# Moving sums, low halves and a table load in the weight stream of a transformer block

## The chip, the cores and the metric

The kernel runs on one core of one Trainium2 chip. The metric is the device time of one execution in microseconds. TensorE is called PE below, VectorE DVE, ScalarE ACT, GpSimd POOL and SyncE SP, as the profile does.

## What is computed

Two blocks in a row over 512 tokens of width 1024, in float32. All that matters for this change lies in the first part of the first block:

```python
mod = c_act @ w_ada[l] + b_ada[l]          # 6 vectors of 1024; c_act = silu(c)
shift1, scale1, gate1, shift2, scale2, gate2 = jnp.split(mod, N_MOD, axis=-1)
h = modulate(rms_norm(x, norm1_g[l]), shift1, scale1)
proj = h @ w_in[l]
q, k, v, g_ret, u, sv, gate_a, gate_b = jnp.split(proj, IN_SPLITS, axis=-1)
q = rotary(q, pos); k = rotary(k, pos)     # heads, scale of k left out
y_ret = head_norm(retention(q, k, v), ret_gn_g[l])
branch_a = (jax.nn.silu(g_ret) * y_ret) @ w_ret_out[l]
y_sgu = spatial_gating(gelu(u), gelu(sv), ...)
branch_b = y_sgu @ w_sgu_out[l]
merged = sigmoid(gate_a) * branch_a + sigmoid(gate_b) * branch_b
x = x + gate1[:, None, :] * (merged @ w_out[l])
```

After it come a lookup among 16384 experts (most of the time) and a second block of two layers, whose own modulation vectors (two conditions, `c_2` and `c_ctx_2`) are products of the same kind with `w_mod`.

## The kernel before

**Weight stream.** All weights come as chunks of 128 by 1024 floats (512 KB), in one order that `make_plan` writes down, and SP loads them one by one into a ring `WR` of `SLOTS` = 4 places. `load(n)` (L641) waits until chunk n-4 has been used. There are two kinds of chunk. A *product chunk* (a "split" in the code) is taken apart for PE: ACT writes its rounded high half `WH` (`high`, L1205) and DVE the rest `WL` (`low`, L1623); after that its place in `WR` is free (`w_split`). `WH` and `WL` have four places of their own, which are free when PE has finished with them. Each product is three matmuls, high by high, high by low and low by high. A *modulation chunk* holds 128 outputs of a modulation vector and never goes to PE: DVE multiplies it by the condition and sums (`mod_sums`, L1635), after which its place is free (`mod_used`). The first 48 of the 96 modulation chunks take one such instruction each, the others two (L1641 and L1643), since they serve two conditions.

**Order of the stream.** 16 modulation chunks come first, since `h` needs shift1 and scale1. The others are strewn between the product chunks by `p.mod(...)` in the plan: one behind each of the eight `qk` chunks, two behind each of the eight `v` chunks, two behind each of the first four `sv` chunks and one behind each of the last four, one behind each chunk of `g_ret`, `u`, `gate_a`, `ret_out`, `gate_b` and `sgu_out`, until 96 are reached. The stages are worked off in this order by PE. `v` and `sv` (function `token_rows`) work in four pairs: a pair of chunks is multiplied with all 512 tokens in four banks, and needs both of its chunks taken apart. Between `v` and `sv` stand the retention scores `s` and values `y`, which need no chunk.

**Order on an engine.** Every engine runs its instructions in the order of the code. Before ACT or DVE reads the bank of a job, `ahead` makes it take all chunks apart up to two behind the newest product chunk of that job (`LOOK` = 2). So the `high` of both chunks of the next `v` pair stands on ACT ahead of its reads of this pair, and the `low` of the first two `sv` chunks stands on DVE ahead of the scores. `streamed(n)` is what DVE does for product chunk n, in this order: the sums of all modulation chunks that lie before it in the stream, then its `low`.

**Start.** ACT's queue asks for the condition `cond`, the vectors `vec`, four constants (`small_loaded`) and the input `XT`; after the squares for the norm it asks for the rotary and decay tables (`tab`, 1.5 MB, L1270), then takes the first two product chunks apart and waits for the scales (`mod_ready`) before it writes `XW` and `Hh` (`shift`, L1256 and L1259). DVE waits for `vec` and the constants before its first sum, sums the 16 chunks with parts of the norm between them (`scaled`, L1714), adds the bias (`biased`), makes `scl1`, and then takes apart two chunks and writes `Hl` (`lowered`, L1720). PE begins with `together` (L813), the first two `qk` chunks at once, as the eight tiles of `Hh` and `Hl` come.

Of the kernel before, what the change touches and what calls it, by code (L numbers as in the profile page):

```python
# [8 lines left out]
T = 512  # L9
C = 256  # L10
A = T + C
KD = D // P
# [16 lines left out]
SPREAD = (1, 2, 3, 0)  # L29
SLOTS = 4  # L30
LOOK = 2
MODS, MODS1 = 96, 48
HOTS = 4
TN = 384
SPARSE, DENSE = 3, (0, 1, 2)
# [123 lines left out]
def make_plan():  # L159
    p = Plan()  # L160

    def lin(key, what, owner, n, cols=("x",)):
        for f in range(n):
            p.chunk((key, f), (*what, f))
            for c in cols:
                p.job((key, f, c), owner, [(key, f)] if c == cols[-1] else [])
# [12 lines left out]
            p.job((*key, "to", g), "V" if g in SPREAD[2:] else "A")  # L179

    p.limit = -1
    p.mod(16)
    p.job(("norm1",), "A")
    spreads(("norm1",))
    p.limit = np.inf

    for f in range(10):
        if f < 8:
            p.chunk(("qk", f), ("w_in", 0, f))
            p.mod()  # L190
            p.job(("qk", f), "A", [("qk", f)])
        if f >= 2:
            p.job(("qkp", f - 2), "V")
# [13 lines left out]
    for name, at in (("g_ret", 2048), ("u", 3072)):  # L207
        for f in range(8):
            p.chunk((name, f), ("w_in", at, f))
            p.mod()  # L210
            p.job((name, f, "x"), "A", [(name, f)])
            if name == "g_ret" and f == 1:
                for h in range(RET_H):
                    p.job(("spread", h), "V")
    for f in range(8):
        p.job(("mix", f), "V")
    for gate, at, name in (("gate_a", 5120, "ret_out"), ("gate_b", 6144, "sgu_out")):
        for f in range(9):
# [4 lines left out]
            if f:  # L223
                p.chunk((name, f - 1), ("w_" + name, 0, f - 1))
                p.mod()
                p.job((name, f - 1, "x"), "V", [(name, f - 1)])
    lin("w_out", ("w_out", 0), "V", 8)
    p.job(("norm2",), "A")
    spreads(("norm2",))
    for f in range(17):  # L230
# [187 lines left out]
def build(nc, plan, d, out):  # L418
# [9 lines left out]
    with ctx:  # L428
# [757 lines left out]
        def _(act):  # L1186
# [80 lines left out]
            act.wait_ge(x_loaded, k.at(x_loaded, 16))  # L1267
            for j in range(KD):
                square(XT, XW, j, T)
            dma(tab[:, 0:3072], d["tab1"][:, :]).then_inc(tab_loaded, 16)  # L1270
            root(("norm1",), rt, T, D)
            spread_norm(("norm1",), rt, T)
            for n in range(LOOK):
                high(n)
            split[0] = LOOK
            act.wait_ge(mod_ready, k.next(mod_ready))
            shift(XW, Hh, lambda c, j: scl1[:, j:j + 1], lambda c, j: mod[:, j, 0:1], ("x",), T)
            for dst, src in ((bs, "bs"), (ws.rearrange("p g t -> p (g t)"), "ws"), (lng[:, :], "lng"), (lnb[:, :], "lnb")):
# [334 lines left out]
        def _(dve):  # L1613
# [4 lines left out]
            def low(n):  # L1618

                dve.wait_ge(w_hi, k.at(w_hi, n + 1))  # L1620
                if n >= SLOTS:
                    dve.wait_ge(*k.emptied(filled, v_used, n))
                v.tensor_tensor(WL[:, n % SLOTS, :, :].rearrange("p a b -> p (a b)"),  # L1623
                                WR[:, plan.splits[n] % SLOTS, :, :].rearrange("p a b -> p (a b)"),
                                WH[:, n % SLOTS, :, :].rearrange("p a b -> p (a b)").bitcast(f32),
                                ALU.subtract).then_inc(w_split, k.inc(w_split))
# [20 lines left out]

            def streamed(n):

                while summed_mods[0] < MODS and plan.mods[summed_mods[0]] < plan.splits[n]:  # L1650
                    mod_sums(summed_mods[0])
                    summed_mods[0] += 1
                low(n)

            def ahead(key):

# [26 lines left out]
            for n, g in ((0, 3), (1, 2), (1, 3)):  # L1683
                v.memset(epsx[QUAD * g:QUAD * (g + 1), n:n + 1], QUAD * QUAD * EPS).then_inc(dve_step, k.inc(dve_step))
            dve.wait_ge(vec_loaded, 16)
            dve.wait_ge(small_loaded, k.at(small_loaded, 16 * len(CONSTS)))

            def biased(lo, hi):

                dve.wait_ge(mod_used, hi)  # L1690
                if lo < MODS1:
                    m, bias = mod[:, lo:hi, 0], V("bias", lo, hi - lo)
                else:
                    m, bias = mod[:, lo:hi, 1:3], V("bias", lo, hi - lo).unsqueeze(2).to_broadcast([P, hi - lo, 2])
                v.tensor_tensor(m, m, bias, ALU.add).then_inc(dve_step, k.inc(dve_step))
                dve.wait_ge(*k.own())
# [15 lines left out]
            def scaled(j, x, work, w):  # L1712

                v.tensor_tensor(work[:, j, 0:w], x[:, j, 0:w], rt[:, 0:w], ALU.mult)\  # L1714
                    .then_inc(xr_ready, k.inc(xr_ready))

            def lowered(j, work, hi, lo, w):

                dve.wait_ge(t_hi, k.next(t_hi))
                v.tensor_tensor(lo[:, j, 0:w], work[:, j, 0:w], hi[:, j, 0:w].bitcast(f32),  # L1720
                                ALU.subtract).then_inc(h_ready, k.inc(h_ready))
# [8 lines left out]
                    if j >= 3:  # L1730
                        lowered(j - 3, work, hi, lo, w)

            for f in range(16):
                mod_sums(f)
                summed_mods[0] += 1
                if f == NORM1_AT:
                    inverted(("norm1",), rt, T)
                if f == NORM1_AT + 1:
                    spread_norm(("norm1",), rt, T)
                if f > NORM1_AT + 1:  # L1740
                    scaled(f - NORM1_AT - 2, XT, XW, T)
            biased(0, 16)
            v1(scl1[:, :], mod[:, 8:16, 0], 1.0, V("norm1", 0, 8), ALU.add, ALU.mult)\
                .then_inc(mod_ready, k.inc(mod_ready))
            for j in range(16 - NORM1_AT - 2, KD):
                scaled(j, XT, XW, T)
            for n in range(LOOK):
                streamed(n)
            split[0] = LOOK
            for j in range(KD):  # L1750
                lowered(j, XW, Hh, Hl, T)

            dve.wait_ge(tab_loaded, k.at(tab_loaded, 16))
            for f in range(8):
# [755 lines left out]
```

## Time and profile before

| | us |
|---|---|
| median of 3 runs | 3556.45 (3555.76 to 3560.99) |
| the profiled execution | 3556.28 |
| its span in the trace | 3554.4 |
| PE busy | 3404.8 |
| DVE busy | 2224.8 |
| ACT busy | 1471.7 |
| POOL busy | 631.4 |

The profile's times are those of one execution, counted from the start of its span. A page of the profile shows the busy time of each engine, the chain of work that ended last, and the costliest groups of instructions. The trace behind it can be read instruction by instruction, and for every one it names what ended the idle time before it. The first 560 us are the part of the first block that the change touches.

### The profile page before, as it was taken

To read this page: it belongs to the slowest core of one execution; us is meant where nothing else is said; L and a number is where in the kernel's file an instruction comes from. 1 tells how busy PE (TensorE), PEld (TensorE's weight loads), DVE (VectorE), ACT (ScalarE), POOL (GpSimd) and SP (SyncE) were. 2 spreads that over 40 slices of the span, in tenths; PEclk is the share of its full clock that TensorE was granted. 3 is DMA by queue.
4 is the path that set the end of the run, shared out by engine and by line. 5 is a ranking of instruction groups with operands and counts; after the bars stand their busy time and mean duration, and the time that the engine had idled before them with its cause. 6 is when DMAs were issued, how large, how long until landed. Compare 5 with 4: busy or idle time off the path is not lost.

```text
span 3554.4 us, 51348 instructions
## 1 busy us (share of the span) xinstructions
PE 3404.8 (96%) x19633; PEld 2956.6 (83%) x19633; DVE 2224.8 (63%) x4546; ACT 1471.7 (41%) x2577; POOL 631.4 (18%) x549
## 2 busy tenths in 40 slices
PE   5999999999999999999999999999999889999997
PEld 4878887999999999999986678778888666777886
DVE  6587765799896668888873652473333346447443
ACT  3233234356767643333343541362122345435222
POOL 0000000037788834443410000000000000000000
PEclk8999999999999999999999999999999899999999
DMA  7545643379889999999952012101221311221222
GB/s 276 194 144 168 202 146 113 115 234 301 293 290 340 293 323 387 361 354 377 390 209 77 31 43 71 37 19 60 66 66 54 114 46 36 78 66 43 94 96 101
DMA packets 219874, 595.84 MB, mean 168 GB/s; under 512 B 17776, under 2 KB 101360, under 8 KB 216176
## 3 DMA queue, kind: packets, MB, share of 16 engines
q1 hardware_dynamic: 159312, 405.84, 33.3%
q0 software_dynamic: 36864, 134.23, 10.9%
q10 hardware_dynamic: 23456, 52.48, 3.9%
q8 instruction: 158, 2.59, 0.3%
q14 instruction: 84, 0.69, 0.1%
HBM read 531.67 MB, written 60.82 MB: 167 GB/s over the span
## 4 chain that ended last, share of the span: by engine, by line
PE 89%; DVE 6%; DMA 2%; ACT 1%; issue 1%; POOL 0%; ACTq 0%; DVEq 0%
PE bank L788 66%; PE bank L988 14%; PE bank L1112 2%; PE bank L957 2%; PE bank L1098 2%; PE bank L813 1%; DMA rows<-in_urows,rk 1%; DMA WR<-in_weights 0%; PE bank L875 0%; DVE SrowA L2214 0%; DVE WL L1623 0%; DVE X L2362 0%; PE bank L945 0%; DVE OF L2359 0%; ACT X2W L1256 0%
## 5 line engine op out<-in xcount | busy, mean ns | idle before, releaser
L1623 DVE TENSOR_TENSOR WL<-WR,WH 128x1024 fp32r<-128x1024 f32 x512 | 628.3, 1228 | 540.0 <-ACT WH L1205 484.9
L1205 ACT ACTIVATE WH<-WR 128x1024 fp32r<-128x1024 f32 x512 | 538.2, 1059 | 580.1 <-PE bank L988 294.2
L788 PE MATMUL bank<-H2h,WH 128*128 128x512 f32 (+1 forms) x1624 | 579.3, 357 | 4.5 <-DVE H2l L1676 4.5
L788 PE MATMUL bank<-H2h,WL 128*128 128x512 f32 (+1 forms) x1624 | 574.5, 354 | 0.0
L788 PE MATMUL bank<-H2l,WH 128*128 128x512 f32 (+1 forms) x1624 | 573.9, 353 | 0.0
L788 PE MATMUL bank<-Hh,WH 128*128 128x384 f32 (+1 forms) x1440 | 517.7, 359 | 5.8 <-DVE WL L1623 5.8
L788 PE MATMUL bank<-Hh,WL 128*128 128x384 f32 (+1 forms) x1440 | 505.7, 351 | 0.0
L788 PE MATMUL bank<-Hl,WH 128*128 128x384 f32 (+1 forms) x1440 | 505.6, 351 | 0.0
L988 PE MATMUL bank<-ah,WH 128*128 128x384 f32 x1024 | 344.4, 336 | 9.0 <-issue 4.5
L788 PEld LDWEIGHTS bank<-H2h,WH 128*128 128x128 f32 x1624 | 308.4, 190 | 50.1 <-issue 7.7
L788 PEld LDWEIGHTS bank<-H2h,WL 128*128 128x128 f32 x1624 | 308.4, 190 | 43.5 <-issue 1.9
L988 PE MATMUL bank<-al,WH 128*128 128x384 f32 x1024 | 344.0, 336 | 0.0
L988 PE MATMUL bank<-ah,WL 128*128 128x384 f32 x1024 | 343.9, 336 | 0.0
L788 PEld LDWEIGHTS bank<-H2l,WH 128*128 128x128 f32 x1624 | 307.8, 190 | 42.3
L719 POOL DMA_INDIRECT rows<-in_urows,rk x128 | 157.8, 1233 | 847.0 <-DVE rk L2026 656.7
L788 PEld LDWEIGHTS bank<-Hh,WH 128*128 128x128 f32 x1440 | 271.6, 189 | 25.3 <-DVE WL L1623 6.7
L788 PEld LDWEIGHTS bank<-Hh,WL 128*128 128x128 f32 x1440 | 271.6, 189 | 16.8 <-issue 1.2
L788 PEld LDWEIGHTS bank<-Hl,WH 128*128 128x128 f32 x1440 | 271.1, 188 | 16.5
L735 POOL TENSOR_SCALAR hotB<-iota,KT 128x128 f32<-128x128 f32 x288 | 283.8, 997 | 2.8
L719 POOL DMA_INDIRECT rows<-in_vrows,rk x128 | 188.9, 1476 | 278.4 <-DVE acc L2043 254.7
L988 PEld LDWEIGHTS bank<-ah,WH 128*128 128x128 f32 x1024 | 193.6, 189 | 10.4 <-issue 5.9
L988 PEld LDWEIGHTS bank<-ah,WL 128*128 128x128 f32 x1024 | 193.5, 189 | 0.0
(363 smaller groups left out, 5557.3 us busy)
## 6 DMA issues: line engine op xcount, KB each, us to landing
WR<-in_weights SPq DMA_DIRECT2D x498, 512.0 KB
WR<-in_vrows SPq DMA_DIRECT2D x128, 512.0 KB
gelu_by_expert<-geU ACTq DMA_DIRECT2D x128, 192.0 KB
gates_by_expert<-tab SPq DMA_DIRECT2D x24, 1024.0 KB
geV<-gelu_by_expert SPq DMA_DIRECT2D x32, 768.0 KB
Gt<-gates_by_expert SPq DMA_DIRECT2D x14, 1536.0 KB
x_kept<-X ACTq DMA_DIRECT2D x2, 3072.0 KB, 10.5
X<-x_kept ACTq DMA_DIRECT2D x2, 3072.0 KB, 12.0
```

The source lines that it names most:

```text
L719: nc.gpsimd.indirect_dma_start(rows[:, i % ROWS, :], None, d[table][:, :], bass.IndirectOffsetOnAxis(ap=expert[:, pick:pick + 1].bitcast(u ...
L735: nc.gpsimd.tensor_scalar(hotB[:, n % HOTS, t, :], consts["iota128"][:, :], KT[:, tt % 2, 1, c:c + 1], None, ALU.is_equal)\
L788: yield nc.tensor.matmul(b[0:rows, out_cols], a, r, start=n == 0, stop=n == len(pairs) - 1)
L813: last = nc.tensor.matmul(b, a, r, start=j == 0 and n == 0, stop=j == KD - 1 and n == 2)
L957: yield nc.tensor.matmul(col(b, t), hotB[:, n % HOTS, t, :], hotA[:, n % HOTS, t, :], start=True, stop=True)
L988: mm = nc.tensor.matmul(bank[sums[dd].bank][:, 0:TN], a, r, start=c == 0 and n == 0, stop=c == NK - 1 and n == 2)
L1098: yield nc.tensor.transpose(col(b, t - t0), col(Srow[kind][u % 4], t), consts["ident"][:, :])
L1112: yield nc.tensor.matmul(b[p0:p0 + VB, 0:P], v_[:, t, 0:VB], PT[kind][:, u % 2, n_, :], start=n_ < 2, stop=n_ >= len(tiles) - 2)
L1205: act.activation(WH[:, n % SLOTS, :, :].rearrange("p a b -> p (a b)"), WR[:, c % SLOTS, :, :].rearrange("p a b -> p (a b)"), ACT.Copy)\
L1623: v.tensor_tensor(WL[:, n % SLOTS, :, :].rearrange("p a b -> p (a b)"), WR[:, plan.splits[n] % SLOTS, :, :].rearrange("p a b -> p (a b)"), ...
```

## The change

Nothing is computed otherwise. Four things move.

1. `streamed(n)`: the `low` of product chunk n comes before the sums of the modulation chunks that lie ahead of it in the stream.
2. The plan: the first product chunk goes ahead of the 16th modulation chunk, the second right behind that; the modulation chunks behind the first two `qk` chunks and behind the first six `g_ret` chunks are gone from there. They come later, since the numbering just runs on: `v` has sums 22 to 37 (24 to 39 before), `sv` 38 to 49 (40 to 51), `g_ret` 50 and 51 (52 to 59), `u` 52 to 59 (60 to 67), the last four places of the `gate_b` stage carry one again, and so do the first four `w_out` chunks. Sums from number 48 on are the double ones, so `sv` has two of them where it had four.
3. DVE's start: it waits for `vec` alone before the first sum, for the constants only after `Hl` is written. `low(0)` and two `scaled` stand ahead of the 16th sum; the other six `scaled` are strewn between the `lowered`.
4. ACT's start: `tab` is asked for behind `high(0)` and `high(1)`.

```diff
-    p.mod(16)
+    p.mod(MODS0 - 1)
     p.job(("norm1",), "A")
...
+    p.chunk(("qk", 0), ("w_in", 0, 0))
+    p.mod()
+    p.chunk(("qk", 1), ("w_in", 0, 1))
     for f in range(10):
         if f < 8:
-            p.chunk(("qk", f), ("w_in", 0, f))
-            p.mod()
+            if f >= 2:
+                p.chunk(("qk", f), ("w_in", 0, f))
+                p.mod()
...
             p.chunk((name, f), ("w_in", at, f))
-            p.mod()
+            if name == "u" or f >= 6:
+                p.mod()
...
-    lin("w_out", ("w_out", 0), "V", 8)
+    for f in range(8):
+        p.chunk(("w_out", f), ("w_out", 0, f))
+        p.mod()
+        p.job(("w_out", f, "x"), "V", [("w_out", f)])
...
-            dma(tab[:, 0:3072], d["tab1"][:, :]).then_inc(tab_loaded, 16)
             root(("norm1",), rt, T, D)
             spread_norm(("norm1",), rt, T)
             for n in range(LOOK):
                 high(n)
             split[0] = LOOK
+            dma(tab[:, 0:3072], d["tab1"][:, :]).then_inc(tab_loaded, 16)
             act.wait_ge(mod_ready, k.next(mod_ready))
...
             def streamed(n):
 
+                low(n)
                 while summed_mods[0] < MODS and plan.mods[summed_mods[0]] < plan.splits[n]:
                     mod_sums(summed_mods[0])
                     summed_mods[0] += 1
-                low(n)
...
             dve.wait_ge(vec_loaded, 16)
-            dve.wait_ge(small_loaded, k.at(small_loaded, 16 * len(CONSTS)))
...
-            for f in range(16):
+            for f in range(MODS0):
+                if f == MODS0 - 1:
+                    for j in range(2):
+                        scaled(j, XT, XW, T)
+                    low(0)
                 mod_sums(f)
...
-                if f > NORM1_AT + 1:
-                    scaled(f - NORM1_AT - 2, XT, XW, T)
-            biased(0, 16)
+            biased(0, MODS0)
             v1(scl1[:, :], mod[:, 8:16, 0], 1.0, V("norm1", 0, 8), ALU.add, ALU.mult)\
                 .then_inc(mod_ready, k.inc(mod_ready))
-            for j in range(16 - NORM1_AT - 2, KD):
-                scaled(j, XT, XW, T)
-            for n in range(LOOK):
-                streamed(n)
+            low(1)
             split[0] = LOOK
             for j in range(KD):
+                if j + 2 < KD:
+                    scaled(j + 2, XT, XW, T)
                 lowered(j, XW, Hh, Hl, T)
+            dve.wait_ge(small_loaded, k.at(small_loaded, 16 * len(CONSTS)))
```

What stands in a row on DVE at the start, before the change, from the eleventh sum to the first writes of `Hl` (L1635 are the sums, L1623 the low halves, L1714 `scaled`, L1720 `lowered`):

```order
L1635 SCALAR_TENSOR_TENSOR WR,mod<-WR,cond 128x1024
L1714 TENSOR_TENSOR XW<-XT,rt 128x512
L1695 TENSOR_TENSOR mod<-mod,vec 128x16
L1743 SCALAR_TENSOR_TENSOR scl<-mod,vec 128x8
L1714 TENSOR_TENSOR XW<-XT,rt 128x512 x3
L1623 TENSOR_TENSOR WL<-WR,WH 128x1024
L1635 SCALAR_TENSOR_TENSOR WR,mod<-WR,cond 128x1024
L1623 TENSOR_TENSOR WL<-WR,WH 128x1024
L1720 TENSOR_TENSOR Hl<-XW,Hh 128x512 x8
```

And with the change (sums now L1643, low halves L1631, `scaled` L1721, `lowered` L1727):

```order
L1643 SCALAR_TENSOR_TENSOR WR,mod<-WR,cond 128x1024 x4
L1721 TENSOR_TENSOR XW<-XT,rt 128x512 x2
L1631 TENSOR_TENSOR WL<-WR,WH 128x1024
L1643 SCALAR_TENSOR_TENSOR WR,mod<-WR,cond 128x1024
L1702 TENSOR_TENSOR mod<-mod,vec 128x16
L1752 SCALAR_TENSOR_TENSOR scl<-mod,vec 128x8
L1631 TENSOR_TENSOR WL<-WR,WH 128x1024
L1721 TENSOR_TENSOR XW<-XT,rt 128x512
L1727 TENSOR_TENSOR Hl<-XW,Hh 128x512
```

The 17th sum is gone from this place, and the scales (`scl`) stand behind three `scaled` less and one low half more.

DVE in the `v` stage before the change, where it comes from the last rotary product of `kT` (L1762):

```order
L1762 TENSOR_TENSOR kT<-kT,G_63 128x512
L1635 SCALAR_TENSOR_TENSOR WR,mod<-WR,cond 128x1024 x2
L1623 TENSOR_TENSOR WL<-WR,WH 128x1024
L1635 SCALAR_TENSOR_TENSOR WR,mod<-WR,cond 128x1024 x2
L1623 TENSOR_TENSOR WL<-WR,WH 128x1024
```

The same place with the change (L1771 is the rotary product):

```order
L1771 TENSOR_TENSOR kT<-kT,G_63 128x512
L1631 TENSOR_TENSOR WL<-WR,WH 128x1024
L1643 SCALAR_TENSOR_TENSOR WR,mod<-WR,cond 128x1024 x2
L1631 TENSOR_TENSOR WL<-WR,WH 128x1024
L1643 SCALAR_TENSOR_TENSOR WR,mod<-WR,cond 128x1024 x2
```

The pair of sums that freed two places of the ring ahead of a low half now stands behind it, eight times in a row here.

DVE at the head of the `g_ret` stage before the change, behind the reciprocal of the variances (L1797); `SV`, `yT` and `lng` are the normalised rows, the retention output and a gain:

```order
L1797 RECIPROCAL ST<-ST 128x512
L1641 SCALAR_TENSOR_TENSOR unread,mod<-WR,tab 128x1024
L1643 SCALAR_TENSOR_TENSOR WR,mod<-WR,tab 128x1024
L1623 TENSOR_TENSOR WL<-WR,WH 128x1024
L1801 TENSOR_TENSOR SV<-SV,lng 128x1024 x4
L1641 SCALAR_TENSOR_TENSOR unread,mod<-WR,tab 128x1024
L1643 SCALAR_TENSOR_TENSOR WR,mod<-WR,tab 128x1024
L1623 TENSOR_TENSOR WL<-WR,WH 128x1024
L1808 SCALAR_TENSOR_TENSOR yT_61<-yT_61,vec,bank 128x512 x8
```

With the change:

```order
L1806 RECIPROCAL ST<-ST 128x512
L1631 TENSOR_TENSOR WL<-WR,WH 128x1024
L1810 TENSOR_TENSOR SV<-SV,lng 128x1024 x4
L1631 TENSOR_TENSOR WL<-WR,WH 128x1024
L1817 SCALAR_TENSOR_TENSOR yT_61<-yT_61,vec,bank 128x512 x8
```

Four of these double-length sum instructions are gone from here, and two more behind.

## Rows read from the trace of the kernel before

**Rows 1.** the page's head: span, and busy time, share of the span and instructions of PE.

```profile
span 3554.4 us, 51348 instructions
PE 3404.8 (96%) x19633; PEld 2956.6 (83%) x19633; DVE 2224.8 (63%) x4546; ACT 1471.7 (41%) x2577; POOL 631.4 (18%) x549
```

**Rows 2.** timeline of the start; start us, us, engine line op out<-in [idle before <-what ended it].

```profile
11.35 1.23 DVE L1635 SCALAR_TENSOR_TENSOR WR<-WR,cond 128x1024 f32<-128x1024 f32 x1 [9.88 <-DMA iota<-in_consts]
...
16.07 0.35 ACTq L1270 DMA_DIRECT2D tab<-in_tab  x1
...
40.44 0.17 DVE L1743 SCALAR_TENSOR_TENSOR scl<-mod,vec 128x8 f32<-128x8 f32 x1
...
42.99 1.06 ACT L1205 ACTIVATE WH<-WR 128x1024 fp32r<-128x1024 f32 x1 [2.79 <-DMA WR<-in_weights]
...
46.58 0.77 PE L813 MATMUL bank<-Hh,WH 128*128 128x512 f32 x1 [15.76 <-DVE Hl L1720]
```

**Rows 3.** a 5 us window; busy PE, PEld, DVE, ACT, POOL, granted PE clock, DMA share, GB/s.

```profile
25.00:30.00 5.00, 0.00 (x0) 0.00 (x0) 4.60 (x8) 0.00 (x0) 0.00 (x0) 0.50 0.99 358
```

**Rows 4.** DMA issues of the first 100 us; KB each, median us to landing.

```profile
tab<-in_tab ACTq DMA_DIRECT2D x1, 1536.0 KB, 9.4
vec<-in_vec ACTq DMA_DIRECT2D x1, 105.0 KB, 6.7
```

**Rows 5.** timeline of the v stage, DVE first, then ACT; columns as in rows 2.

```profile
104.04 0.09 DVE L1635 DVE_READ_ACCUMULATOR WR<-WR,cond 128x1 f32 x1
105.19 0.09 DVE L1635 DVE_READ_ACCUMULATOR WR<-WR,cond 128x1 f32 x1
108.06 1.23 DVE L1635 SCALAR_TENSOR_TENSOR WR<-WR,cond 128x1024 f32<-128x1024 f32 x1 [0.50 <-DMA WR<-in_weights]
...
124.06 0.08 DVE L1635 DVE_READ_ACCUMULATOR WR<-WR,cond 128x1 f32 x1
...
109.86 1.06 ACT L1205 ACTIVATE WH<-WR 128x1024 fp32r<-128x1024 f32 x1 [8.66 <-DMA WR<-in_weights]
130.97 1.06 ACT L1205 ACTIVATE WH<-WR 128x1024 fp32r<-128x1024 f32 x1 [5.57 <-DMA WR<-in_weights]
```

**Rows 6.** chain of work that ended last; start us, us, what.

```profile
105.30 4.54 DMA WR<-in_weights
...
112.28 34.80 PE bank L788 x288
147.11 0.39 ACT Vr L1231
```

**Rows 7.** timeline of DVE in the sv stage; columns as in rows 2.

```profile
177.61 0.08 DVE L1635 DVE_READ_ACCUMULATOR WR<-WR,cond 128x1 f32 x1
182.27 1.23 DVE L1635 SCALAR_TENSOR_TENSOR WR<-WR,cond 128x1024 f32<-128x1024 f32 x1 [0.71 <-DMA WR<-in_weights]
```

**Rows 8.** timeline of PE at its two waits behind the sv stage; columns as in rows 2.

```profile
259.96 0.80 PE L788 MATMUL bank<-Hh,WH 128*128 128x512 f32 x1 [5.57 <-DVE WL L1623]
...
265.68 0.49 PE L788 MATMUL bank<-Hh,WL 128*128 128x512 f32 x1
...
266.70 0.40 PE L788 MATMUL bank<-Hl,WH 128*128 128x512 f32 x1
...
267.63 0.39 PE L788 MATMUL bank<-Hh,WH 128*128 128x512 f32 x1
...
349.11 0.50 PE L788 MATMUL bank<-yh,WH 128*128 128x512 f32 x1 [2.75 <-DVE WL L1623]
```

**Rows 9.** 2 us windows behind the first of these waits; columns as in rows 3.

```profile
262.00:264.00 2.00, 2.00 (x7) 1.54 (x6) 2.00 (x5) 0.00 (x0) 0.00 (x0) 0.50 0.64 233
266.00:268.00 2.00, 2.00 (x10) 1.64 (x9) 2.00 (x5) 0.00 (x0) 0.00 (x0) 1.00 0.85 285
```

**Rows 10.** timeline of DVE at the two low halves that PE waits for there; columns as in rows 2.

```profile
258.69 1.22 DVE L1623 TENSOR_TENSOR WL<-WR,WH 128x1024 fp32r<-128x1024 f32 x1
...
347.83 1.23 DVE L1623 TENSOR_TENSOR WL<-WR,WH 128x1024 fp32r<-128x1024 f32 x1
```

More of the change, by code:

```diff
@@ L31 @@
 LOOK = 2
-MODS, MODS1 = 96, 48
+MODS0, MODS1, MODS = 16, 48, 96
 HOTS = 4
```

## Prediction, made before the changed kernel had run

> **What bounds the kernel now.** The page's head comes first: PE is busy for 3404.8 of 3554.4 us [rows 1], so all that any edit can win is in the 150 us in which PE stands still, and an edit loses where it makes PE stand still longer. The change touches the first 560 us. There PE's own waits were read next. It first multiplies a `qk` chunk at 46.58 us [rows 2]; then it has to wait ahead of the second pair of `v`, which the chain reaches at 112.28 by way of a load [rows 6], 5.57 us in `g_ret` and 2.75 us before `ret_out` [rows 8]. The last two are waits for a low half `WL`, and so is the first, at the end of that load. The last view is the timeline of DVE and ACT at these places, with what ended their idle time.
>
> The quantity to get hold of is the time from the release of a place in the ring to the landing of the chunk that is loaded into it. In the `v` stage a sum's accumulator is read at 104.04 for 0.09 us; the next chunk for that place is seen to land when a waiting sum starts at 108.06, so 3.9 us. The sum that ends at 105.28 releases the place of a product chunk, for which the chain shows 4.54 us [rows 5, 6]. In `sv` the same reads 177.69 to 182.27, 4.6 us [rows 7]. With more loads under way it was longer: 124.14 to 130.97, 6.8 us [rows 5]. I take **4.5**, since the new order has two or three loads out, as at 105; 3.9 and 5.2 are the ends for the sum.
>
> **The change part by part.**
>
> *Start.* Before, DVE starts its first sum at 11.35, having waited for the last constant [rows 2]. Now it waits for `vec`, issued at about 1.2 and 6.7 us on its way [rows 4]: about 8.0. That alone gives little, since the DMA engines are saturated from 5 us on (share 0.99 still at 25 to 30, [rows 3]). What helps more is that `tab`, 1536 KB [rows 4], is no longer asked for at 16.07 [rows 2], among the weights: at 358 GB/s [rows 3] it is worth 4.4 us. Worked forward with a chunk every 1.46 us (524 KB at that rate), the 12th to 14th sums end at 29.7, 30.8 and 32.0 and release the places of `qk` 0, the 16th modulation chunk and `qk` 1, which land at about 34, 35 and 36.5. Two `scaled`, `low(0)` and the last sum then end at about 37.2 and the scales at 37.5 (40.44 before). ACT, which only began `XW` at 44.0, behind the `WH` of a chunk that had come at 42.99 [rows 2], begins at about 38; `Hl` and PE follow 2.6 us behind (44.0 to 46.58), at 40.5. Gain **6.1 us**, between 4.5 (both landings 1 us later) and 8 (the DMA at the 400 GB/s of a mixed load). The tables then fall between 38 and 47, on a ring that has nothing urgent; DVE first waits for them ahead of `low(2)` near 51. Cover left: 4 us. The strewn `scaled` cost nothing: one and a `lowered` are 1.2 us, ACT needs 1.4 for a tile.
>
> *Low half ahead of the sums, two modulation chunks between product chunks.* This is the term that decides. Call the stream a, b, s, c, d, t, e, f. Place numbers repeat after four, so t is loaded into the place of b, and SP can ask for it only when b has been summed. Before, a and b were summed as they landed, while s was still coming. Now they wait for `low(s)`. So from one low half to the next there stand in a row: two sums at 1.15 (104.04 to 105.19, [rows 5]) 2.3, the load 4.5, `WH` 1.1 [rows 5], `WL` 1.2 [rows 10], together **9.1 us**. PE takes 34.80 us for three pairs [rows 6], 5.8 for a chunk. The 3.3 us between are no longer hidden. Reckoned on: in the `qk` stage (one sum per chunk, 8.0 us for two chunks against 12 of PE) PE is not reached. The first `v` pair runs from 93.2, with its second low half done at 89.9 and that one's sums at 92.2. From there the low halves end at 99.0, 108.0, 117.1, 126.2, 135.2, 144.3, 153.4 and 162.4; PE's second, third and fourth pairs start at 108.0, 126.2 and 144.3 (before 112.28, and 11.6 and 23.2 behind that). The last two low halves are those of the first `sv` pair, yet DVE must do them before the scores and ACT their `WH` before it reads the fourth `v` pair. The scores therefore start at about 162.5 where they started behind the read at 147.11 [rows 6], which lasts 0.39, at 147.5. With the start's 6.1 us in it this is 15.0 later: price **21.1 us** (3.9 us a load: 16.5; 5.2: 26.7).
>
> *The same in `sv`.* From the end of `y` the four low halves of its second and third pair come at 2.8, 11.9, 21.0 and 28.9 us. PE wants the second pair at 11.6 and the third at 23.2; the third starts 5.7 late, of which 0.3 come with the second. Behind them the stream has one modulation chunk between product chunks and PE is not reached. Price **5.7 us** (3 to 8).
>
> *PE's clock.* The wait of 5.57 us had a second price. The granted clock was 0.50 at 262 to 264 and 1.00 at 266 to 268 [rows 9], that is 1.2 and 2.4 GHz, and the 14th matmul behind the wait starts 5.72 us after the first, where later ones stand 0.23 apart [rows 8]: 5.72 less 13 times 0.23 is 2.7 us. The new waits ahead of the scores (about 4 us) and of the third `sv` pair (5.7) are of that kind and lie on the path; those inside `v` are covered by the ring. Price **4 us**, between 0 and 5.4.
>
> *No sums in `g_ret`.* Of the sums there, 12 instructions, four and two more stood ahead of the low half that ended PE's wait at 259.96 [rows 8, 10]. Without them that low half is done at 254.1 in the same reckoning, and PE asks for it at 254.4. Gain **8.3 us**: 5.57 of wait and 2.7 of clock; what is late next is that same low half, with 0.3 us to spare, so 5.5 at the low end.
>
> *`ret_out`.* The low half at 347.83 [rows 10] comes two sums, 2.3 us, earlier, and PE's wait of 2.75 shrinks as much: **2.3 us** gained. Its `WH` is done before 345.5, so nothing else holds it. Where one double sum stands between product chunks (`u`, `gate`), sum 2.3, load behind another load 5.7 (3.9 and the 1.8 between the landings at 108.06 and 109.86), 1.1 and 1.2 make 10.3 us for two chunks, against 10.9 of PE: nothing, but close. The four sums in `w_out` lie beside 5.4 us of PE each.
>
> Sum: -6.1 + 21.1 + 5.7 + 4 - 8.3 - 2.3 = **+14.1 us**. The profiled execution, 3556.28, is the median of the runs within 0.2, so 3570.
>
> **The rivals.** (1) *The load is shorter when few are out.* The ring now idles more than half the time, and the 3.9 us of a first load [rows 5] speak for some of it; the 4.54 and 4.6 with just one load ahead speak against. 11 loads stand in the chain, so each 1 us less gives 11 back, and at 3.2 the sum is +14.1 - 14.3, no change: 3556. The Trainium skill has such a figure (DMA: Bandwidth & Descriptors, "Anatomy of one DMA"): about 2.0 us fixed and the bytes at 436 GB/s for a DMA issued by GpSimd, from which 512 KB would be an estimated 3.2 us. These loads are SP's, and no row here shows one that short.
>
> (2) *The ring does not hold PE*, because loads run ahead in a way that I overlook, and only the gains stay: 3556.3 - 6.1 - 8.3 - 2.3 = 3539.6. The point from which it decides is a load of under 1.2 us (5.8 less 4.6), which the landings contradict; what speaks for it is only that I derived the order of releases from the plan.
>
> (3) *The stages with one double sum are held as well.* With 0.6 us more in a load (as the 6.8 us shows is possible with more out) two chunks cost 11.5 instead of 10.9, over the 20 such pairs of `u` and the gates 12 us: 3582.
>
> (4) *The start gives nothing*, because the DMA engines and not the order set the 16 sums, and `x` takes what the tables leave: 3576.
>
> **How the numbers follow.** Forecast 0.55 (3562 to 3580), (1) 0.13, (2) 0.10, (3) 0.12, (4) 0.10. What a measurement can tell from no change is 0.2%, 7 us, so 3549 to 3563.5 is "same". Faster has (2) and a little of (1): 0.12. Same has most of (1) and the low tail of the forecast, where a load takes 3.9 and the clock costs nothing (14.1 - 7 - 4 = +3): 0.17. Slower has the rest: 0.71. The forecast's own range is 3562 to 3580. The range leaves out (2) and the far end of (3): 3550 to 3584.
>
> **What would show it.** In the new trace the first `L813` matmul should stand near 40.5; the low halves of the `v` stage 9 us apart, each behind a `WH` that waited for a load, with two sums between; PE waiting 4, 6 and 6 us ahead of the second to fourth `v` pair, 4 ahead of the scores and 5 to 6 ahead of the third `sv` pair, with a clock of 0.50 behind the long ones; no wait of 5 us in `g_ret`, and some 0.4 instead of 2.75 before `ret_out`. I am wrong if low halves in `v` follow each other in 6 us or less, or if loads land 3.2 us after their release.

## The result, and the profile after the change

The changed kernel takes 3577.6 us (median of 4 runs, 3576.4 to 3580.1), the kernel before 3558.0 beside it: ratio 1.0057, interval 1.0044 to 1.0070. It is **slower by 20 us**. Forecast were 3570 and a range of 3550 to 3584.

The two profiled executions, 3578.63 and 3556.28, lie 22.35 apart, and their spans 22.4, so the traces show the loss whole. The head of the page after, to be read beside [rows 1]:

```profile
span 3576.8 us, 51335 instructions
PE 3414.8 (95%) x19633; PEld 2962.0 (83%) x19633; DVE 2225.7 (62%) x4546; ACT 1473.4 (41%) x2577; POOL 631.1 (18%) x549
```

PE is busy 10 us longer with as many instructions, and stands still 12 us longer. The loss arises in the first 260 us, where it reaches 30.7, and 8.9 of that have come back by 371, as these stations of PE show (by its timeline in both traces):

| station | before | after | difference |
|---|---|---|---|
| first product | 46.58 | 41.06 | -5.5 |
| first product of the scores | 147.54 | 167.52 | +20.0 |
| end of the retention values | 173.71 | 195.78 | +22.1 |
| last sum of the gated products (DVE `yT`) | 226.68 | 257.38 | +30.7 |
| first product of the first `ret_out` chunk | 349.11 | 370.89 | +21.8 |
| first product of the expert stage | 1295.3 | 1317.6 | +22.3 |
| end of the span | 3554.4 | 3576.8 | +22.4 |

**Start.** The timeline, in the columns of [rows 2] and beside those rows:

```profile
7.85 1.23 DVE L1643 SCALAR_TENSOR_TENSOR WR<-WR,cond 128x1024 f32<-128x1024 f32 x1 [6.38 <-DMA vec<-in_vec]
17.31 1.23 DVE L1643 SCALAR_TENSOR_TENSOR WR<-WR,cond 128x1024 f32<-128x1024 f32 x1 [4.79 <-DMA WR<-in_weights]
...
38.41 0.17 DVE L1752 SCALAR_TENSOR_TENSOR scl<-mod,vec 128x8 f32<-128x8 f32 x1
41.06 0.77 PE L821 MATMUL bank<-Hh,WH 128*128 128x512 f32 x1 [13.53 <-DVE Hl L1727]
```

The first sum starts 3.5 us sooner, but the DVE then waits 4.79 for a chunk. What the scales gain is 2.0 (40.44 to 38.41), and ACT, which finds its `WH` done, turns that into 5.5 at PE.

**The v stage.** DVE's timeline around two of the low halves, beside [rows 5]:

```profile
118.26 1.23 DVE L1631 TENSOR_TENSOR WL<-WR,WH 128x1024 fp32r<-128x1024 f32 x1 [6.49 <-ACT WH L1213]
119.40 1.22 DVE L1643 SCALAR_TENSOR_TENSOR WR<-WR,cond 128x1024 f32<-128x1024 f32 x1
...
120.54 1.22 DVE L1643 SCALAR_TENSOR_TENSOR WR<-WR,cond 128x1024 f32<-128x1024 f32 x1
...
127.90 1.23 DVE L1631 TENSOR_TENSOR WL<-WR,WH 128x1024 fp32r<-128x1024 f32 x1 [6.13 <-ACT WH L1213]
```

One low half, two sums, 6 us of nothing, the next low half: 9.64 us. The chain that ended last names what fills the 6 us (start us, us, what):

```profile
119.40 2.38 DVE WR L1643 x4
121.80 4.99 DMA WR<-in_weights
...
126.81 1.07 ACT WH L1213
...
129.04 2.38 DVE WR L1643 x4
131.44 5.33 DMA WR<-in_weights
```

Before, this chain touched a load once in the whole stage [rows 6]; now it does so eight times, and its loads are 5.30, 5.02, 5.35, 4.99, 5.33, 4.57, 4.35 and 5.62 us long, 5.07 in the mean. The low halves start at 98.57, 108.25, 118.26, 127.90, 137.89, 147.12, 156.12 and 166.40: **9.7 us** apart, where PE needs a chunk each 5.8. What waited for what from 60 to 260 us (engine line waited for: us in total, times, longest):

```profile
ACT WH L1213 <- DMA WR<-in_weights: 89.3, 15, 9.2
DVE WL L1631 <- ACT WH L1213: 81.8, 18, 9.7
...
PE bank L796 <- DVE WL L1631: 22.1, 5, 6.4
```

Before, the first of these was 33.3 us in 8 waits. At the head of the scores, behind the last wait of the `sv` stage and at 260 us, the windows show the clock (columns as in [rows 3]):

```profile
165.00:170.00 5.00, 2.48 (x3) 1.17 (x4) 3.60 (x6) 2.15 (x5) 0.00 (x0) 0.50 0.10 34
170.00:175.00 5.00, 5.00 (x17) 3.22 (x16) 3.43 (x8) 0.00 (x0) 0.00 (x0) 0.83 0.82 285
...
225.00:230.00 5.00, 4.80 (x23) 4.83 (x24) 3.61 (x6) 2.42 (x6) 0.00 (x0) 0.53 0.57 168
260.00:265.00 5.00, 5.00 (x23) 2.11 (x24) 3.02 (x4) 1.89 (x3) 0.00 (x0) 0.66 0.00 0
```

**Behind the v stage.** The answers to [rows 8]: the wait of 5.57 us at the head of `g_ret` is gone, and the one of 2.75 ahead of `ret_out` is 0.45. But PE is at a lower clock while it forms the norm's sums ahead of `g_ret` (3.15 us for 16 matmuls; 1.92 before, behind the same wait of 2.56):

```profile
259.90 3.15 PE L904 MATMUL bank<-XW,ones 128*32 128x512 f32 x16 [2.56 <-ACT XW L1314]
262.98 0.80 PE L796 MATMUL bank<-Hh,WH 128*128 128x512 f32 x1
...
370.89 0.50 PE L796 MATMUL bank<-yh,WH 128*128 128x512 f32 x1 [0.45 <-DVE WL L1631]
```

### The profile page after: what moved, and what is told of

The parts are those of the page before. It is cut to its first block, busy times and chain, and to the rows that moved or that the text cites. A ratio compares the mean times of both kernels' runs of the same rounds, so it can differ in the third digit from the quotient of the medians.

```text
span 3576.8 us, 51335 instructions
## 1 busy us (share of the span) xinstructions
PE 3414.8 (95%) x19633; PEld 2962.0 (83%) x19633; DVE 2225.7 (62%) x4546; ACT 1473.4 (41%) x2577; POOL 631.1 (18%) x549
## 4 chain that ended last, share of the span: by engine, by line
PE 87%; DVE 6%; DMA 4%; ACT 2%; issue 1%; POOL 0%; DVEq 0%; ACTq 0%
PE bank L796 64%; PE bank L996 13%; PE bank L1120 3%; PE bank L965 2%; PE bank L1106 2%; DMA WR<-in_weights 2%; PE bank L821 1%; DMA rows<-in_urows,rk 1%; DVE WR L1643 1%; PE bank L883 0%; ACT WH L1213 0%; DVE SrowA L2223 0%; DVE WL L1631 0%; DVE X L2371 0%; PE bank L953 0%
## 5 line engine op out<-in xcount | busy, mean ns | idle before, releaser
L1631 DVE TENSOR_TENSOR WL<-WR,WH 128x1024 fp32r<-128x1024 f32 x512 | 628.8, 1229 | 614.5 <-ACT WH L1213 560.0
L996 PEld LDWEIGHTS bank<-al,WH 128*128 128x128 f32 x1024 | 193.4, 189 | 0.0
```

The source lines that it names most:

```text
L996: mm = nc.tensor.matmul(bank[sums[dd].bank][:, 0:TN], a, r, start=c == 0 and n == 0, stop=c == NK - 1 and n == 2)
```

## Experiments

The theory under test is the ring: in the stages with two modulation chunks between product chunks, a load can be asked for only when the sums are done, the sums stand behind the low half, that behind `WH`, and that behind the load before. The rivals are that the start or the moved tables bring the loss, that the six moved sums do, and, as to the mechanism, that loads or DVE alone hold the stage.

### Undo the order alone

The changed kernel with the low half behind the sums again.

```diff
             def streamed(n):
-                low(n)
                 while summed_mods[0] < MODS and plan.mods[summed_mods[0]] < plan.splits[n]:
                     mod_sums(summed_mods[0])
                     summed_mods[0] += 1
+                low(n)
```

> The changed kernel with one thing undone: from the third chunk on, the low half of a chunk stands behind the modulation sums again (start, tables and plan of the change are kept). Theory (the ring of load, WH, low half and two sums holds the stage of the v products): the low halves of that stage come under 2.5 us behind their WH only at its end, the first product of the scores starts near 142 instead of 167.5, the stage of the gated sums loses the 8.6 it gained in cost, and the time is 3577.6 - 25.5 - 5.7 - 2.9 = about 3543, or up to 3547 if the gain of 2.3 ahead of the projections goes with it and the clock falls elsewhere. Rival A (the start or the moved tables make the loss, by traffic that runs on into the v products): it stays within 5 of 3577. Rival B (the plan, which moved six sums, makes it): it stays there too, and the loads of the v stage stand as in the changed kernel.

Measured: **3544.1 us** (3542.0 to 3549.8, 5 runs), ratio to the kernel before 0.9964 (0.9951 to 0.9978). That is 33.5 less than the changed kernel, within 1.2 us of what was reckoned for the ring (3543), and neither of the two rivals allows it. Behind one wait of 1.5 us, ahead of the second `v` pair, PE runs through the stage, and the scores start at 142.54:

```profile
142.10 0.39 ACT Vr L1239
...
142.54 4.58 PE bank L796 x16
```

### The order alone, on the kernel before

> The kernel before with one thing of the change: the low half of each chunk from the third on ahead of its modulation sums; start, tables and plan stay as before. Theory: the ring alone makes the loss. The scores start 25 later than 147.5, near 173, the gated sums cost 6 to 9 more, the last projection of the block is 2.3 quicker, and the time is about 3558 + 25.5 + 7 - 2.3 = 3588. The changed kernel is 10 to 12 quicker than this one by its other two parts. Rival A (start or tables) or B (plan): within 5 of 3558.

```diff
             def streamed(n):
+                low(n)
                 while summed_mods[0] < MODS and plan.mods[summed_mods[0]] < plan.splits[n]:
                     mod_sums(summed_mods[0])
                     summed_mods[0] += 1
-                low(n)
```

Measured: **3586.1 us** (3582.4 to 3587.9), ratio 1.0077 (1.0064 to 1.0091). The eight loads in its chain take 4.8 to 5.7 us (mean 5.14), and the scores start at 173.36, 25.8 later than before:

```profile
166.25 4.89 DMA WR<-in_weights
...
172.22 1.10 ACT Vr L1231 x4
173.36 6.28 PE bank L788 x16
```

So one line that swaps two steps makes the loss by itself. The rest of the change wins only 8.5 us back from it, less than the 10 to 12 expected: with the low half first, PE's wait at the head of `g_ret` is already 2.8 us instead of 5.57, so that part of what the plan wins is won here too.

### The start alone and the plan alone

The first takes from the change only the start (waits for constants, tables, order of the first chunks), the second only the six sums that leave `g_ret` for `w_out`; both keep the old `streamed`.

```diff
-            p.mod()
+            if name == "u" or f >= 6:
+                p.mod()
...
-    lin("w_out", ("w_out", 0), "V", 8)
+    for f in range(8):
+        p.chunk(("w_out", f), ("w_out", 0, f))
+        p.mod()
+        p.job(("w_out", f, "x"), "V", [("w_out", f)])
```

> The kernel before with the start of the change alone: constants awaited where they are used, tables asked for behind the weight chunks, sixteen chunks and the order of the first ones, their low halves among the scale products. The plan of the later products and the order of sums and low halves from the third chunk on stay as before. Theory: the first product starts near 41.1 instead of 46.6 and the v products keep their pace, so 3558 - 5.5 = about 3552. Rival A (the start moves traffic or sums into the v products and is itself the cause of the loss): the scores start later than 147.5 and the time is above 3560. Rival C (what the start gains is lost again at the first wait, since the modulation chunks bind there): 3558.

> The kernel before with the six moved sums alone (from ahead of the first six chunks of the retention gate to those of the output projection); start and order of sums and low halves stay. Theory: the wait of 5.57 at the start of the gate's products and the clock that falls with it go, 6.6 to 8.3 less, and the chunks of the output projection carry the sums under products: about 3558 - 7 = 3551, or 3554 if half the sums show ahead of the output projection when the low halves stand behind them, where before there was a wait of 2.75. Rival B (the moved sums cost more than they save): above 3559.

Measured: the start alone 3552.4 us (3551.0 to 3558.0, 11 runs), ratio 0.9987 (0.9978 to 0.9996); the plan alone 3550.35 (3546.8 to 3554.7, 11 runs), ratio 0.9981 (0.9972 to 0.9990). That is 5.3 and 7.3 us less than before, as expected, and together with the 33.5 of the order they close: 3557.7 - 5.3 - 7.3 = 3545.1 against 3544.1 measured for both. In the plan's kernel PE's wait of 5.57 is not among its waits from 60 to 420 us:

```profile
PE bank L792 <- DVE WL L1627: 4.5, 2, 2.7
PE bank L900 <- ACT XW L1310: 2.6, 1, 2.6
PE bank L792 <- ACT Vr L1235: 0.5, 1, 0.5
```

(The two waits in the first row are 1.8 us in `v` and 2.7 ahead of `ret_out`.) The profiled execution of the start's kernel, 3556.4, lies 4.0 above its median; the last section has one cause.

### The v stage alone mended

Here only the ten chunks of `v` and of the first `sv` pair have their sums first.

```diff
-                low(n)
+                first = plan.chunk_at[("v", 0)] <= plan.splits[n] <= plan.chunk_at[("sv", 1)]
+                if not first:
+                    low(n)
                 while summed_mods[0] < MODS and plan.mods[summed_mods[0]] < plan.splits[n]:
...
+                if first:
+                    low(n)
```

> The changed kernel with the low half behind the sums again for the ten chunks of the v products and of the first pair of the gated sums alone; everywhere else the low half stays first. It parts the two places. Theory: the v stage loses its whole price of 25.5 (the scores start near 142.5), and the gated sums keep theirs, which is 8.6 with the clock in it: 3577.6 - 25.5 = 3552, that is 8.6 above the kernel with all sums first (3544.1), less the 2.3 ahead of the output projection: 3550 to 3552. Rival G (the wait in the gated sums was left over by the v stage, whose loads ran late into it): with v mended the gated sums cost nothing, 3542.

Measured: **3550.9 us** (3545.6 to 3554.8, 11 runs), ratio 0.9980 (0.9971 to 0.9989): 26.7 less than the changed kernel. The scores start at 142.37, and the gated sums lose by themselves what they lost in the changed kernel. Their last sum starts at 230.40, where the kernel with all sums first has 221.67: 8.7 us for the same work. Two waits of PE, 1.14 and 5.38, are 6.5 of it, and the rest is its clock behind the second (0.59 and 0.73 where it had been 1.00):

```profile
195.00:200.00 5.00, 1.71 (x8) 1.74 (x9) 2.37 (x3) 4.00 (x7) 0.00 (x0) 0.59 0.65 217
200.00:205.00 5.00, 5.00 (x34) 5.00 (x34) 2.37 (x3) 0.71 (x2) 0.00 (x0) 0.73 0.77 236
```

The two stages are two independent rings; rival G of this run is out.

### One sum on either side

> The changed kernel, but where two sums wait for a chunk one of them stands ahead of the low half and one behind it, all on the same chunks. Theory: the ring loses one sum of 1.15 from each cycle, 9.7 becomes 8.55 in the eight chunks of the v stage (9.2 less), and three or four cycles of the gated sums lose the same (3 to 4 less): about 3577.6 - 13 = 3565, between 3562 and 3567; the low halves of the v stage stand 8.5 apart. Rival E (the ring is closed by the loads alone, which take longer the more often they are asked for, so that the cycle stays at 9.7): 3577. Rival F (what decides is whether any sum is behind the low half, since the vector engine alone sets the pace with its total work): 3577 too, with no idle time of that engine ahead of the low halves.

```diff
             def streamed(n):
 
+                waiting = sum(1 for c in plan.mods[summed_mods[0]:] if c < plan.splits[n])
+                if waiting >= 2:
+                    mod_sums(summed_mods[0])
+                    summed_mods[0] += 1
                 low(n)
```

Measured: **3550.8 us** (3549.2 to 3553.8, 11 runs), ratio 0.9981 (0.9972 to 0.9990). It gains 26.8 us, twice what I expected. The chain shows why; the cycle is 7.3 us, not 8.55:

```profile
115.33 1.24 DVE WR L1643 x2
116.59 3.65 DMA WR<-in_weights
...
120.26 1.07 ACT WH L1213
...
122.50 1.24 DVE WR L1643 x2
123.75 3.81 DMA WR<-in_weights
```

One sum of 1.15 us is gone from the cycle, as expected, but the load is also shorter: 3.98, 3.81, 3.65, 3.81, 3.61, 4.00 and 3.67 in place of 5.07. SP's queue shows what differs. SP asks in the order of the stream, so the place that the low half frees is filled last, though it is free first. In the changed kernel both sums stand behind the low half. The load into the first one's place goes out 1.14 us ahead of the chain's load, and the one into the low half's place 0.37 behind it:

```profile
120.66 0.33 SPq L649 DMA_DIRECT2D WR<-in_weights  x1
121.80 0.33 SPq L649 DMA_DIRECT2D WR<-in_weights  x1
122.17 0.43 SPq L649 DMA_DIRECT2D WR<-in_weights  x1
```

The second is the load of 4.99 above. In the kernel of this experiment the first sum is done ahead of the low half, so its load has gone out 6.2 us earlier and has landed, at 115.60, when the chain's load is asked for. The chain's load is now the first of its group (in the first of the seven cycles, 3.98, one still stands 2.28 us ahead of it):

```profile
116.59 0.33 SPq L649 DMA_DIRECT2D WR<-in_weights  x1
116.96 0.43 SPq L649 DMA_DIRECT2D WR<-in_weights  x1
117.73 0.33 SPq L649 DMA_DIRECT2D WR<-in_weights  x1
```

The windows show the batch. The changed kernel, from the end of a low half on (columns as in [rows 3]):

```profile
119.00:121.00 2.00, 2.00 (x19) 2.00 (x19) 2.00 (x4) 0.00 (x0) 0.00 (x0) 1.00 0.04 8
121.00:123.00 2.00, 1.82 (x16) 1.62 (x14) 0.77 (x2) 0.00 (x0) 0.00 (x0) 1.00 0.68 186
123.00:125.00 2.00, 0.00 (x0) 0.00 (x0) 0.00 (x0) 0.00 (x0) 0.00 (x0) 1.00 0.85 274
125.00:127.00 2.00, 0.00 (x0) 0.00 (x0) 0.00 (x0) 0.19 (x1) 0.00 (x0) 1.00 0.82 293
```

The kernel with one sum on either side, likewise:

```profile
115.00:117.00 2.00, 2.00 (x19) 2.00 (x18) 2.00 (x4) 0.00 (x0) 0.00 (x0) 1.00 0.01 4
117.00:119.00 2.00, 2.00 (x19) 2.00 (x19) 0.70 (x2) 0.00 (x0) 0.00 (x0) 1.00 0.72 199
119.00:121.00 2.00, 2.00 (x19) 2.00 (x18) 0.00 (x0) 0.74 (x1) 0.00 (x0) 1.00 0.99 363
```

For about 1 us behind the first request nothing moves. Then 186, 274 and 293 GB/s over 2 us each are 1.5 MB, nearly three chunks, and the chain's load lands at 126.8. In the kernel of this experiment it has landed at 120.24, after some 0.85 MB (199 GB/s over 2 us and 363 over 1.2). In both the chain's load shares the engines with what is asked for just around it, and with one load ahead of it more has to move first. The shorter cycle frees the `sv` stage too: PE has no wait there at all. Rivals E and F are out, since the cycle fell by more than the sum.

### Half of each load

This kernel is the changed one, but in the `v` stage it loads only the first 512 columns of each row, so that products there use old weights; all instructions stay. 

> The changed kernel with loads of half the size in one stage: the chunks asked for in the stage of the v products bring the first 512 columns of each row and not the rest, so part of the computation uses old weights; every instruction stays. It measures of what the 5.07 from release to landing consist. If it is all by bytes (the queue's rate), a load takes 2.5 and the cycle falls from 9.7 to 7.2. If 2.0 of it is fixed, as the Trainium skill has it (page DMA: Bandwidth & Descriptors, section Anatomy of one DMA), a load takes 3.5 and the cycle is 8.2. If the fixed part is larger, 3 or more, a load takes 4 and the cycle is 8.7. Theory: the stage gets shorter by eight times what a load gets shorter, 9 to 20 in all, with the time at 3558 to 3569. Rival E (other traffic or the vector engine holds the cycle): the cycle stays at 9.7.

```diff
+                half = D // 2 if plan.chunk_at[("v", 1)] < n < plan.chunk_at[("sv", 0)] else D
-                sp.dma_start(WR[:, n % SLOTS, :, :].rearrange("p a b -> p (a b)"), src)\
+                sp.dma_start(WR[:, n % SLOTS, :, :].rearrange("p a b -> p (a b)")[:, 0:half], src[:, 0:half])\
```

Measured: 3568.3 us in its one run, 9.3 less than the changed kernel and at the low end of the 9 to 20 expected. In its chain one cycle, from load to load, reads

```profile
122.04 2.38 DVE WR L1644 x4
124.44 3.06 DMA WR<-in_weights
...
132.16 3.07 DMA WR<-in_weights
```

The load takes 3.1 instead of 5.07 and the cycle 7.7 instead of 9.7: it falls by what the load falls, and no more. (Four loads of the chain, from 108.75 to 132.16, have this size and take 3.06 to 3.30; the next two, 4.32 and 5.40, bring the first `sv` pair and are full ones.) The batch of three carries 1.5 chunks fewer, so the 2.0 us come to an estimated 1.3 us a chunk. The other 3.1 do not all scale with the bytes. By the Trainium skill (DMA: Bandwidth & Descriptors, "Anatomy of one DMA": about 2.0 us fixed and the bytes at 436 GB/s, for a DMA that GpSimd issues, where these are SP's) a 512 KB load alone is an estimated 3.2 us. The shortest in these chains are 3.52 (the kernel with `v` mended, at 192.33) and 3.56 (the changed kernel at 83.89). Nothing had been asked for in the 5.9 us ahead of either, and the next went out 1.14 and 0.37 behind. So the page's sum is 0.3 under a load that is asked for first, and 1.9 under the mean of those with another 1.14 ahead.

### Sums first only where two wait

The version the runs point to: sums ahead where two or more wait, low half ahead elsewhere.

```diff
-                low(n)
+                waiting = sum(1 for c in plan.mods[summed_mods[0]:] if c < plan.splits[n])
+                if waiting < 2:
+                    low(n)
                 while summed_mods[0] < MODS and plan.mods[summed_mods[0]] < plan.splits[n]:
...
+                if waiting >= 2:
+                    low(n)
```

> The changed kernel, but where two or more modulation sums wait for a chunk they go first, as before, and only where at most one waits is the low half first. Theory: the ring of two sums is gone from the v products and the gated sums, and the 2.3 ahead of the output projection stays, so it is about 2 under the kernel with all sums first (3544.1): near 3542, and faster than both the changed kernel and the one before. Rival A (a single sum behind a low half also holds loads, in the u and gate products): slower than 3544. Rival D (the 2.3 of the output projection only moves a wait): 3544.

Measured: **3541.5 us** (3539.0 to 3550.5, 5 runs), ratio 0.9951 (0.9938 to 0.9965). It beats both kernels. PE's wait ahead of `ret_out` is 0.5 in its trace and 2.7 with all sums first, as expected, but the intervals of the two ratios overlap, so that the times don't part them. Against rival D (the 2.3 us only move a wait) stands that up to 560 us no other wait is longer for it. Rival A is out by the trace: from `g_ret` to the end of the gates PE has no wait for a low half longer than the 0.5 us, so `u` and the gates with their single sums are not held.

### The tables early again

The same kernel with `tab` asked for ahead of the first two `WH`, as before the change.

```diff
+            dma(tab[:, 0:3072], d["tab1"][:, :]).then_inc(tab_loaded, 16)
             root(("norm1",), rt, T, D)
             spread_norm(("norm1",), rt, T)
             for n in range(LOOK):
                 high(n)
             split[0] = LOOK
-            dma(tab[:, 0:3072], d["tab1"][:, :]).then_inc(tab_loaded, 16)
```

> The quickest kernel so far (all of the change, with sums first where two of them wait; 3541.5), but with the tables asked for where they were before the change, ahead of the first two weight chunks to be taken apart. It tells which part of the new start brings the 5.5. Prediction of record: the tables are worth 4.4 of it and the earlier first sum little, so the first product starts near 45.5 instead of 41.1, and the time is 3546. Rival H (the earlier first sum and the order of the low halves bring it): the first product stays within 1 of 41.1, and the time at 3541.5.

Measured: 3545.9 us (3542.0 to 3548.0), ratio 0.9963 (0.9949 to 0.9977). The medians are 4.4 apart, but the intervals overlap. The trace is the better witness. One sum waits 2.77 us for its chunk, where from 18 us on the sums of the kernel without this edit wait 0.54 at most, and the first product is later:

```profile
26.02 1.23 DVE L1643 SCALAR_TENSOR_TENSOR WR<-WR,cond 128x1024 f32<-128x1024 f32 x1 [2.77 <-DMA WR<-in_weights]
...
43.95 0.76 PE L821 MATMUL bank<-Hh,WH 128*128 128x512 f32 x1 [13.68 <-DVE Hl L1731]
```

The first product starts at 43.95, and at 41.03 to 42.05 in the seven other kernels with the new start. So by the traces the tables are worth 2 to 3 us of the 5.5, and the rest of the new start as much. The truth lies between the prediction of record (4.4) and rival H.

## Why the prediction was right, and where its sizes were off

The mechanism, its places and its sign were right; the time was 7.6 us too low. Term by term, by the stations above (they are reached at 22.4, and the last 0.6 are spread over the rest):

| term | forecast | traces | kernel that isolates it |
|---|---|---|---|
| start | -6.1 | -5.5 | -5.3 |
| `v` stage | +21.1 | +25.5 | -26.7 when mended |
| `sv` stage and clock | +5.7 + 4 | +8.6 + 2.1 + 1.2 | +8.7 with `v` mended |
| no sums in `g_ret` | -8.3 | -7.8 | -7.3 |
| `ret_out` | -2.3 | -2.3 | |
| sum | +14.1 | +21.8 | |

- **The load was the term that was mis-sized.** I took 4.5 us from the load at 105.30, which was asked for 1.15 us behind another [rows 5, 6]. Those of the new chain stand just so behind another, and measured 5.07. What differs is the load behind: it follows at 0.37 us instead of 1.14, since its place has been free since the low half. The half loads show that the bytes of the batch count; that the closer follower makes the 0.5 us is not shown, as no run has it alone. The cycle of 9.1 became 9.7, and over eight cycles that is 4.8 of the 7.7 us that the sum is short. The 6.8 us of [rows 5] was a warning that the neighbours count: that load had two asked for ahead of it, at 1.14 and 2.28.
- **The clock cost more, and at a place I had not named.** The 4 us of record were to come from two waits. The one ahead of the scores cost 2.1 by the clock; in `sv` two waits, 1.5 and 4.7, and the clock behind them came to 8.6, where 5.7 stood for the waits alone; and the clock fell once more, to 0.66 from 260 to 265, for 1.2 us more.
- **Start**: the forecast for the scales was 37.5, measured 38.41, and for PE 40.5, measured 41.06. The first sum came at 7.85, as reckoned (8.0), and bought less than its 3.5 us, since the chunks weren't there. The tables bought 2 to 3, not 4.4.
- **`g_ret` and `ret_out`**: the cover of 0.3 us was seen right. PE's wait fell from 5.57 to nothing that the trace shows, and from 2.75 to 0.45.
- **The rivals.** Rival 1 (a load of 3.2 us, 3556) fell: the loads of the chain were longer than those of the rows, although the engines stood idle between the batches. Rival 2 (the ring doesn't hold PE, 3539.6) has another use: the kernel in which it doesn't, 3541.5, is what the change is worth without its one bad line. Rival 3 (`u` and the gates held) fell with that same kernel. Rival 4 (the start gives nothing) fell with the start's own kernel; that its time, 3576, lies nearest to the measured one is chance, since the start gave 5.5 and the load and the clock took more.

## What to carry to other kernels

In a ring of buffers, ask of every reordering who frees a place, and what stands between the landing of one load and the release for the next: work that was done while a load was under way costs nothing, and the same work behind the consumer of that load is added to every turn. A load in such a chain is priced by what is asked for just ahead of it and behind it, so a row with other neighbours doesn't serve. The order in which places come free is not the order in which they are filled: here the place that was free first was filled last. When an edit has parts with different signs, part them: here one line lost 33.5 us and the rest won 12.6.

## What the runs showed of the hardware beside this

- **A load of 512 KB has a price by its neighbours.** From release to landing, in the chains: with nothing asked for in the 5.9 us ahead of it, 3.5 to 3.8 us where one load follows at 0.37 or two at 1.14 and 1.5, and 3.6 to 4.0 where two follow at 0.37 and 1.14; with one asked for 1.14 ahead and the next 0.37 behind, 4.4 to 5.6 in the changed kernel and 4.6 to 5.7 in the one with the order alone.
- **One load of the `v` stage has two lengths in equal code.** The load that ends PE's wait ahead of the second pair (4.54 in [rows 6]) took 4.62 and 4.51 us in two of the kernels with sums first, and 7.39, 7.47 and 6.85 in three others, in which the code up to there is the same or nearly so, with a PE wait of 3.7 to 4.3 instead of 1.4 to 1.5. In all five SP asked for the loads around it at the same distances, within 0.4 us. With the clock behind the wait, PE took 104.8 to 106.5 us from its first product to the scores in those three, and 101.0 to 101.3 in the two. That covers the 4.0 us by which the profiled execution of the start alone lies above its median, but not the 9.0 of the best kernel's: this one also took 3210.3 us from `ret_out` on, 2.9 more than the kernel with all sums first, and the cause of that is open too. In the best kernel's chain the load is

```profile
99.30 7.39 DMA WR<-in_weights
```

and in that of the kernel with all sums first

```profile
100.21 4.62 DMA WR<-in_weights
```

In the long case the engines stay at work for other chunks (258, 344 and 377 GB/s in the three us from 101) while the awaited one is late. Why its bytes come last in some executions and not in others, I did not find out; it is open, and with it 3.5 to 5.5 us of the way to the scores.
- **The length of a wait alone didn't tell whether clock was lost.** From 100 to 120 us the granted clock was 1.00 where PE's wait ahead of the second `v` pair was 1.5 us (all sums first), and 0.91 and 0.83 where it was 4.2 and 4.3 (the best kernel, the start alone). But behind the wait of 2.56 ahead of the norm's sums, which all kernels have, the 16 matmuls took 1.92 us in the kernel before and in the one with all sums first, 3.15 in the changed kernel and 3.55 in the one with one sum on either side. Behind the 4.6 us ahead of the scores and the 5.4 of the kernel with `v` mended the clock was 0.50 to 0.83, which cost an estimated 2.1 and 2.2 us (from the stations, less the waits).
